# Differential-attention mixer of a two-layer transformer block: ScalarE takes over emptying the dense PSUM banks, and layer 0's modulation units are dealt 12 and 12 instead of 14 and 10

## The reference

```python
def adaln_params(cond, w_mod, b_mod):
    return jnp.split(jax.nn.silu(cond) @ w_mod + b_mod, 6, axis=-1)

def modulate(x, g, shift, scale):
    return rmsnorm(x, g) * (1.0 + scale) + shift

def attend(q, k, v):                       # differential attention, 4 heads, 2 maps of 32 each
    s = jnp.einsum('bhmqd,bhmkd->bhmqk', q, k).astype(jnp.float32) * scale
    a = jax.nn.softmax(s, axis=-1)
    a = a[:, :, 0] - lam * a[:, :, 1]
    return jnp.einsum('bhqk,bhkd->bhqd', a.astype(v.dtype), v)
...
for layer in range(DEPTH):
    mod_l = [m[:, None, :] for m in adaln_params(c, w_mod[layer], b_mod[layer])]
    mod_c = adaln_params(c_ctx, w_mod[layer], b_mod[layer])
    p_l = split_cols(modulate(x, norm1_g[layer], mod_l[0], mod_l[1]) @ w_in[layer])
    ...
    x = x + mod_l[2] * (jnp.concatenate([a_l, b_l, n_l, w_l], axis=-1) @ w_out[layer])
    x = x + mod_l[5] * squared_relu_mlp(modulate(x, norm2_g[layer], mod_l[3], mod_l[4]),
                                        w_ff1[layer], w_ff2[layer])
```

## Time and profile before

| | |
|---|---|
| median of 3 runs | 2276.91 us (2276.86 to 2279.08) |
| the profiled execution, its own time | 2280.41 us |
| its span, first to last instruction | 2278.6 us |
| PE busy | 2083.6 us (91%) |
| DVE busy | 1017.8 us (45%) |
| ACT busy | 784.8 us (34%) |
| POOL busy | 686.2 us (30%) |
| mean granted clock of TensorE | 0.959 of full |

### The profile page before, as it was taken

One profiled execution on the slowest core, in us unless ns is written; L12 is line 12 of the kernel. 1 busy time (PEld: TensorE's weight loads), 2 busy tenths in 40 slices (PEclk: granted clock), 3 DMA queues, 4 the chain that ended last, 5 costly groups with the idle time before them and its releaser, 6 DMA issues.

```text
span 2278.6 us, 32056 instructions
## 1 busy us (share of the span) xinstructions
PE 2083.6 (91%) x13292; PEld 1734.6 (76%) x13292; DVE 1017.8 (45%) x1791; ACT 784.8 (34%) x1283; POOL 686.2 (30%) x567
## 2 busy tenths in 40 slices
PE   5799898889889899999999988998998888999998
PEld 3578787768777788888888867777787677778787
DVE  2535546855775631212213253445857754121122
ACT  1533323434335621312213153233444355232231
POOL 0230212012751232322322323223024513444442
PEclk9889998989999999999999998999999989999999
DMA  8220010342411121121121123010242311222222
GB/s 287 48 74 19 20 38 19 130 138 83 149 57 56 38 74 56 56 75 56 56 74 56 56 46 76 19 38 19 93 119 93 112 56 56 93 93 93 94 91 74
DMA packets 178353, 169.72 MB, mean 74 GB/s; under 512 B 29393, under 2 KB 174753, under 8 KB 178081
## 3 DMA queue, kind: packets, MB, share of 16 engines
q1 hardware_dynamic: 177408, 164.53, 23.4%
q10 hardware_dynamic: 800, 3.15, 0.4%
HBM read 159.79 MB, written 2.10 MB: 71 GB/s over the span
## 4 chain that ended last, share of the span: by engine, by line
PE 75%; DVE 11%; ACT 6%; issue 3%; SPq 2%; DMA 2%; POOL 1%; DVEq 0%; ACTq 0%; POOLq 0%
PE gp L877 52%; PE sp L1109 3%; PE sp L1260 2%; PE gp L1146 2%; PE tp L1126 2%; PE gp L931 1%; SPq L710 1%; PE sp L1100 1%; POOL HGx_kd L775 1%; DVE small L2174 1%; ACT nt L1458 1%; PE sp L950 1%; PE gp L901 1%; PE op L1126 1%; PE op L1146 1%
## 5 line engine op out<-in xcount | busy, mean ns | idle before, releaser
L788 POOL TENSOR_TENSOR wlo<-raw,whi 128x512 fp32r<-128x512 f32 x386 | 514.2, 1365 | 1306.2 <-ACT whi L1424 1306.1
L877 PE MATMUL gp<-xhi,whi 128*128 128x512 f32 (+1 forms) x1424 | 520.5, 366 | 34.8 <-DVE xlo L1963 21.4
L877 PE MATMUL gp<-xhi,wlo 128*128 128x512 f32 (+1 forms) x1424 | 507.3, 356 | 0.0
L877 PE MATMUL gp<-xlo,whi 128*128 128x512 f32 (+1 forms) x1408 | 503.3, 357 | 0.0
L877 PEld LDWEIGHTS gp<-xhi,whi 128*128 128x128 f32 x1424 | 277.0, 195 | 83.2 <-issue 14.5
L1424 ACT ACTIVATE whi<-raw 128x2048 fp32r<-128x2048 f32 (+1 forms) x100 | 187.3, 1874 | 367.9 <-PE gp L877 356.4
L877 PEld LDWEIGHTS gp<-xhi,wlo 128*128 128x128 f32 x1424 | 276.5, 194 | 39.3
L877 PEld LDWEIGHTS gp<-xlo,whi 128*128 128x128 f32 x1408 | 273.7, 194 | 38.6 <-issue 2.0
L877 PE MATMUL gp<-hhi,whi 128*128 128x512 f32 (+1 forms) x768 | 276.4, 360 | 9.6 <-issue 5.0
L877 PE MATMUL gp<-hlo,whi 128*128 128x512 f32 (+1 forms) x768 | 274.9, 358 | 0.0
L877 PE MATMUL gp<-hhi,wlo 128*128 128x512 f32 (+1 forms) x768 | 274.7, 358 | 0.0
(11 more groups left out here) (361 smaller groups left out, 3249.9 us busy)
## 6 DMA issues: line engine op xcount, KB each, us to landing
raw<-in_w_ff SPq DMA_DIRECT2D x64, 1024.0 KB, 5.3
raw<-in_w_mod SPq DMA_DIRECT2D x48, 1024.0 KB, 5.2
raw<-in_w_in SPq DMA_DIRECT2D x20, 1024.0 KB, 5.1
raw<-in_w_in SPq DMA_DIRECT2D x24, 256.0 KB, 4.5
bias<-e SPq DMA_DIRECT2D x96, 32.0 KB
raw<-in_w_out SPq DMA_DIRECT2D x12, 256.0 KB, 3.1
xin<-in_x ACTq DMA_DIRECT2D x1, 2048.0 KB, 9.6
raw<-in_w_out SPq DMA_DIRECT2D x16, 128.0 KB, 3.2
```

What stands on the lines that cost most here:

```text
L788: nc.gpsimd.tensor_tensor(wlo[:, s % 2, ks, :], raw[:, index[splits[s]] % 2, ks, :], whi[:, s % 2, ks, :].bitcast(F32), ALU.subtract)\
L877: mm = pe.matmul(out, lhs, rhs, start=(i == 0 and j == 0), stop=(i == KT - 1 and j == 2))
```

## The change

Four things, all in the DA and HG stages:

1. In `counts`, DA of layer 0 takes 12 modulation units and HG of layer 0 takes 12 (before 14 and 10). Layer 1 keeps 7 and 9.
2. In HG of layer 0 the units are laid out over 11/12 of the slots (33 of 36) instead of 3/4.
3. In DA of both layers ACT empties the banks of rows, value chunks and query chunks, in a new function `empty(slot)` behind `expo(n+1)` and ahead of the rounding of the next unit.
4. DVE keeps the turns alone, and does a slot's turn ahead of `finish(n+1)`.

```diff
@@ fill_plan @@
-    counts = {("NA", 0): 0, ("SW", 0): 0, ("DA", 0): 14, ("HG", 0): 10, ("NA", 1): 0, ("SW", 1): 0, ("DA", 1): 7, ("HG", 1): 9}
+    counts = {("NA", 0): 0, ("SW", 0): 0, ("DA", 0): 12, ("HG", 0): 12, ("NA", 1): 0, ("SW", 1): 0, ("DA", 1): 7, ("HG", 1): 9}
...
-            span = 3 * n // 4 if m == "HG" else n
+            span = (11 * n // 12 if l == 0 else 3 * n // 4) if m == "HG" else n
@@ ACT @@
+            def empty(slot):
+
+                for u, c in slot:
+                    if c == "turn":
+                        continue
+                    n = N(u, c)
+                    act.wait_ge(group_done, n + 1)
+                    if c == "row":
+                        dst, src = mrow[:, :], bank(n)[:, 0:UC]
+                    elif c[0] == "tok":
+                        dst, src = buf("HG", "v")[:, c[1], :], bank(n)[:, 0:UC]
+                    else:
+                        a, b = SEGS[c[1]]
+                        dst, src = buf("HG", "q1")[:, c[0], a:b], bank(n)[:, 0:b - a]
+                    nc.scalar.activation(dst, src, ACT.Copy).then_inc(bank_free[group_bank[n]], 1)
...
                     if m == "DA":
                         expo(n + 1)
+                        empty(ENDS[m, l][n])
...
                 if m == "DA":
+                    empty(ENDS[m, l][-1])
@@ DVE @@
+            def turns(slot):
+
+                fill((u, c) for u, c in slot if c == "turn")
...
-                    fill(EARLY[m, l][n])
-                    finish(n + 1)
-                    fill(ENDS[m, l][n][len(EARLY[m, l][n]):])
+                    if m == "DA":
+                        turns(ENDS[m, l][n])
+                        finish(n + 1)
+                    else:
+                        fill(EARLY[m, l][n])
+                        finish(n + 1)
+                        fill(ENDS[m, l][n][len(EARLY[m, l][n]):])
                     output(n)
-                fill(ENDS[m, l][-1])
+                if m == "DA":
+                    turns(ENDS[m, l][-1])
+                else:
+                    fill(ENDS[m, l][-1])
```

## The result

| | before | after |
|---|---|---|
| median of 12 runs each | 2278.95 us (2274.79 to 2284.70) | 2267.37 us (2260.45 to 2275.52) |
| the profiled execution | 2280.41 us | 2267.51 us |

The changed kernel is 11.6 us faster; the ratio is 0.9950, 95% interval 0.9935 to 0.9965. The forecast was 2271.6 us with 2268.0 to 2276.5, so the time lies just outside the range, and the change of time is twice the forecast one of 5.3 us. A second set (8 runs, experiment 9) gave 2267.54 us, 10.8 us less than the kernel before beside it.

A forecast was written before the change was run, and what follows sets the result against it. PE, busy 91% of the span, was taken as the bound, with DVE close to second in DA of layer 0. Terms -5.6 (DA layer 0), +1.2 (HG), -0.9 (DA layer 1) took 2276.91 to 2271.6 us, range 2268.0 to 2276.5.

The forecast's parts named there:

- rival B: TensorE's clock, DA of layer 0: a low stretch added (2273.3 to 2275.0 us) or removed (2269.9); chance 0.18.
- Step 1: DA of layer 0: moving emptying from DVE to ACT closes PE waits, 1.7 us saved, bounds 0.9 and 2.3.
- Steps 2 and 3: DA of layer 0: two modulation units leave, 2.9 us saved; slots dealt again close PE waits, 1.0 us saved.
- Step 4: End of DA, layer 0: savings late there worth nothing; load, rounding and subtraction for HGf0 stay 11.2 us.
- Step 5: HG of layer 0: two added units cost net +1.2 us, partly covered by PE waits; bounds +0.5 and +4.4.
- Step 6: DA of layer 1: moving the emptying copies shortens PE waits, 0.9 us saved, bounds 0.3 and 1.0.
- C: DA: ACT becomes the pacer, its added copies delaying transposed probabilities, 14 us in all, 2285.6 us; chance 0.06.
- A: HG of layer 0 takes the gain back, costing +4.4 us, 2274.8 us in all; chance 0.20.
- D: DA: copies were not the cause, waits on mix pass to the next dependence, -2.7 us, 2274.2 us; chance 0.06.

The follow-up runs named there:

- experiment 9: The changed kernel run again with no further edit: 2267.54 us, ratio 0.9952 to the kernel before.
- the emptying alone: Kernel before with only ACT emptying the banks in DA of both layers; units stay 14 and 10, span 3/4: 2275.20 us, ratio 0.9986.
- the deal alone: Kernel before with only 12 and 12 units and the span 11/12 in layer 0, DVE still emptying: 2272.40 us, ratio 0.9975.
- experiment 3: Changed kernel with the span of HG in layer 0 back at 3/4 (12 units in 27 levels): 2267.15 us, ratio 0.9955.
- experiment 4: Changed kernel with the emptying in DA of layer 1 left to DVE: 2267.22 us, ratio 0.9961.
- the three with the last rows early: Changed kernel, layer 0 DA's last two units before the last value chunk: 2270.09 us; also squares before rounding: 2265.26; that plus extra matmuls in two waits: 2268.44.
- 13 units: Changed kernel with 13 units in DA and 11 in HG of layer 0: 2270.51 us, ratio 0.9960.
- experiment 5: Changed kernel, DA of layer 0 with its last two units ahead of the last value chunk, HGf0 rounded behind the last step: 2270.27 us.

## Why the prediction was half the size

The step that failed is the clock. The sum put the change's effect on TensorE's clock at nothing and left it to rival B, at 1.7 us for one stretch with a chance of 0.08. The traces have 6.8 us at low clock in DA of layer 0 where before has 10.3 and 17.0, some 3.4 us of time. The second step is HG, forecast at +1.2 and measured at -0.1. The two terms for DA of layer 0, which make up the prediction's idea, came out within a microsecond.

**Step 1, emptying in DA of layer 0, -1.7.** Right in kind, a little small: the emptying alone gives -2.5 at equal clock, just past the upper bound of 2.3. One reading was wrong. Of the four waits on `mix` two stay, since there the chain that writes `DA_p` ends just before the output copy; taking a copy of 0.42 us from between lets PE arrive earlier as well and wait for the same chain. The 0.90 became 0.31 as said. The 1.01 us for a load, which was to grow, went away with the deal. It varies by itself: 0.32 us in the second trace of before, 0.66 and 2.05 with the emptying alone.

**Steps 2 and 3, the units and the slots, -2.9 and -1.0.** Together -3.9 forecast, -4.1 measured by the deal alone. The waits behind the slots came out as said: before the scores of steps 6 and 8 they closed, and slot 2 opened 0.29 and 0.37 us.

**Step 4, the tail.** `HGf0` still starts a fixed time behind the row that frees its buffer, with 3.50 us of waiting (forecast 3 to 4). The time is 10.5 us and not 11.2, in both traces of after (before 11.2 and 11.3): the load lands 0.7 us sooner. The emptying alone has 10.8 and 10.4 with 14 units. The load ahead of `HGf0`'s was issued 7.2 us before it now (477.88) and 6.1 us in before, which may be why; no run tells.

**Step 5, HG of layer 0, +1.2.** This term had the wrong sign: -0.1. The levels did get longer, by 0.8 us, within the bounds, but not as reasoned. Work of PE grew by 2.5 us, its idle time fell by 1.7. Three waits for which the profile shows no releaser, 1.5 us together, are gone; the 0.89 us that the prediction named is one of them (its row says "issue" and not POOL). The waits for DVE's masked products, of which one was to go, grew from 7.5 us in ten:

```profile
PE sp L1260 <- DVE HG_at L2371: 8.5, 13, 1.5
```

And the later weights of `outA`, which the prediction took to cost nothing, take POOL out of DVE's way and give 0.9 us back (experiment 3).

**Step 6, DA of layer 1, -0.9.** The traces of before and after differ by 1.0 us at equal clock, but experiment 4 puts only 0.4 of it down to the copies.

**Rival B, the clock.** The prediction had one stretch late in DA, worth 1.7 us if it went, and gave that 0.08. Its one trace was the milder of two: the second has three such stretches. In the changed kernel's DA they are gone in six of seven traces, and in the three with the last rows early, 3.4 us on average (low time 10.3 and 17.0 against 6.8). That is the largest missing piece. C and A did not come; D was half right on the waits and wrong on the sum.

**The bounds.** Those of the steps add up to -7.5 and +1.2, not to the -8.5 and 0 that the prediction gives.

**The base.** The three runs shown had 2276.91 us; the twelve have 2278.95, all 98 a median of 2277.6. One to two microseconds of the change of time come from there. As execution times spread by 10 us and more, three values within 2.2 us were luck.

The sum with the measured sizes: -6.1 for DA of layer 0 at equal clock, -3.4 for its low stretches, -0.2 from the squares to `HGf0` (6.50 and 6.59 us before, 6.32 and 6.39 after; the other 0.5 us of the load lie within the 6.1), -0.1 for HG, -1.0 for DA of layer 1, together -10.8 us, against -11.6 and -10.8 measured. That the two agree so well is in part luck. The code behind DA of layer 1, which no edit touches, differs by 5.5 us between the first traces of before and after:

```profile
1680.63:2278.60 597.97, 553.71 (x2888) 453.68 (x2888) 224.59 (x338) 208.00 (x284) 247.53 (x199) 0.96 0.28 89
1673.28:2265.70 592.42, 548.68 (x2888) 449.74 (x2888) 224.57 (x338) 208.07 (x284) 248.98 (x200) 0.97 0.28 90
```

It has 49 us of low clock in before and 39 in after, and the second traces repeat this (598.37 and 592.47 us). But the kernel with the span 3/4, whose DA of layer 1 is the same, has 597.69 again. From the output weights to DA of layer 1 it is 919.78 and 922.70 us before, 924.58 and 922.32 after. So low time outside the stages of the sum moves by more than the sum's error, and the traces don't tell whether the change has a part in it.

**What stays open** is why the stretches go. All thirteen middle stretches of the table begin 0.1 to 1.7 us behind the end of a wait of PE of 0.35 us or more; most such waits have none behind them. The plainest case is step 19, ahead of which PE waits twice in a row. In before and in the changed kernel:

```profile
475.10 0.38 PE L1109 MATMUL sp<-DA_hi,DA_hi 32*128 32x256 f32 x2 [1.15 <-ACT DA_p L1614]
476.71 0.52 PE L1126 MATMUL tp<-cf,DA_p 128*128 128x128 f32 x3 [0.99 <-DVE DA_p L2191]
...
468.60 0.38 PE L1109 MATMUL sp<-DA_hi,DA_hi 32*128 32x256 f32 x2 [1.15 <-ACT DA_p L1630]
470.22 0.52 PE L1126 MATMUL tp<-cf,DA_p 128*128 128x128 f32 x3 [1.00 <-DVE DA_p L2213]
```

In before and the emptying alone this pair ends at 101.5 to 105.4 us behind the first scores, and in all four traces a stretch begins within 1.7 us behind it. In the deal alone the pair ends at 100.8 (none directly behind it) and 99.3 (one at 100). In the changed kernel it ends at 97.4 to 98.1 with the waits as long as before, and nothing follows in six traces of seven; with 13 units it is shorter, ends at 96.6, and a stretch begins at 96. So the size of these waits alone does not decide. That they lie elsewhere now, because the stage ahead of them got shorter, is a guess that fits and that no run tests. If it holds, this part of the gain is no merit of the change's idea, and a further edit ahead can bring a stretch back; 13 and 11 had one.

## What to carry to other kernels

One trace is one draw of the clock: take two or three of the kernel before, list the low stretches of the stage, and price an edit at equal clock first and the stretches apart. A wait can cost more than its own length: filling the one of 3.5 us for `HGf0` made what follows 2 us shorter. When dense work is spread between two stages, count its own cost and also which engine's later work it shifts: here weights that came later were worth 0.9 us, because POOL then paused while DVE made its copies.

## What the runs showed of the hardware

- The same code before DA of layer 0, unchanged in all kernels, had between 48 and 75 us of low clock in 18 traces, and its first scores came between 369.2 and 377.0 us.
- Small DVE copies within SBUF can take 1.2 us instead of 0.2 beside back-to-back subtractions on POOL (experiment 3).
- In one of the 12 executions of experiment 5 (5027.81 us) the granted clock read 1.00 throughout, and yet matmuls took twice their time: 719 ns on average in the largest group, 365 ns in the page of after. The page of that execution:

```profile
span 5026.0 us, 32056 instructions
PE 4942.5 (98%) x13292; PEld 3479.3 (69%) x13292; DVE 974.9 (19%) x1756; ACT 799.1 (16%) x1318; POOL 647.7 (13%) x567
L877 PE MATMUL gp<-xhi,whi 128*128 128x512 f32 (+1 forms) x1424 | 1024.6, 719 | 11.7 <-DVE xlo L1987 4.4
```

DVE and ScalarE worked as fast as ever, so the granted clock does not tell of every slowing of TensorE.
